# The first layer's paired sample steps: the prompt's scores, weight transposes and products in three places of a step instead of two

## The chip, the cores and the metric

The kernel runs on one core of a Trainium2 chip. The metric is the device time of one execution in microseconds (us). The engines are named as in the profile: PE (TensorE, its weight loads apart as PEld), DVE (VectorE), ACT (ScalarE), POOL (GpSimd) and SP (SyncE, here the queue that issues most DMAs; SPq is its sequencer).

## The reference

One inference step of a decoder with two layers, for a prompt group (512 tokens) and a sample group (8 sequences of 8 tokens, each with 2048 tokens in a paged cache). The first layer mixes by a pooling part and a differential attention, four heads, each with two score maps of 64 features:

```
def diff_attn_core(q, ks, vs, masks, lam, lam_init, subln_g):
    logits = jnp.concatenate([jnp.einsum('bqhmd,bkhmd->bhmqk', q, k) for k in ks], axis=-1).astype(jnp.float32) * (HD_B ** -0.5)
    logits = jnp.where(jnp.concatenate(masks, axis=-1), logits, -jnp.inf)
    p = jax.nn.softmax(logits, axis=-1)
    a = p[:, :, 0] - lam * p[:, :, 1]
...
        part = jnp.einsum('bhqk,bkhe->bqhe', a[..., off:off + n].astype(v.dtype), v)
...
    o = rmsnorm(o, subln_g) * (1.0 - lam_init)
```

The prompt attends to itself, causally, in blocks of 128 queries; the samples attend to their cache pages and to themselves. Then come the output projection, an MLP, a second layer (convolution and dilated window attention) and its MLP; these are not touched here.

## The kernel before

Each engine runs its own list of instructions in the order in which the program writes them; semaphores hold an instruction until another engine has done its part. There is no scheduler: what stands next in an engine's list waits, and all behind it on that engine waits too.

The stage of this case is the first layer's attention. The samples are taken in four pairs (j = 0 to 3), and each pair in nine blocks (i = 0 to 8): eight with two cache pages of each sample of the pair, that is four pages of 512 KB, and one with the new tokens. That makes 36 steps, m = 9j + i. On PE a step is: the sample scores (`scores`, L728), the key transposes of the next block's first two pages (`keys`, L714), the value products of the block before (`values`, L748), the key transposes of the next two pages (L714), then a piece of other work, and the transposes of the sample's own weights (`weights`, L736). In the step with i = 7 there are no next keys. DVE and ACT copy the transposed keys from PSUM (L1338 and L1932, every second page each, one PSUM bank for each engine), DVE takes the maximum of the scores (L1348 to L1354), ACT the exponentials (L1942) and the copy of the weights (L1950). SP loads the pages into a ring of four blocks (`kvring`, L431); a slot is free again when the values of the block four before are done.

The other work is the prompt's attention, in 16 items (4 heads by 4 query blocks; n = 4h + qt, and a query block has qt + 1 key blocks). Each item passes through PE three times: scores (L834, PSUM buffer `P0_SCORES`), transposes of the combined weights (L845), products (L852; both in PSUM bank 7). Between them DVE masks and reduces the scores (L1450, L1451), ACT takes the exponentials (L2008), DVE combines the two maps into one (`prompt_combine`, L1462 to L1466, semaphore `p0_a`), ACT copies the transposed weights (L2017, semaphore `p0_at`). DVE copies the result out (L1456) and ACT squares it (L2040).

Which item falls into which step is said by `beside(m, first, stage, last)`: item s runs in step m = first + 7 * s // 4. DVE has three such calls: output of n at first = 4, mask and maximum of s at first = 1, combine of n at first = 2. PE and ACT have before the change a `prompt_stage(s)` at first = 1 that holds the scores (on ACT the exponentials) of item s and, right behind them, the weights of item s - 1; PE's products stand at first = 4, ACT's squares too. In a step PE runs the product first, then the scores, then the weights.

Of the kernel before, what the change touches and what calls it, by code (L numbers as in the profile page):

```python
# [26 lines left out]
ACT = mybir.ActivationFunctionType  # L27
# [3 lines left out]
P = 128  # L31
# [111 lines left out]
def build(nc, a):  # L143

    with ExitStack() as ctx:
# [15 lines left out]
        def at(name, word, words, dt=F32):  # L161
            assert word + words <= total, (name, word + words, total)
            return nc.alloc_sbuf_tensor_at(name, [P, words], dt, offset=base + 4 * word)

        def tiles(t, n, first=0):
            return t[:, first * N:(first + n) * N].rearrange("p (k n) -> p k n", n=N)
# [23 lines left out]
        pk = tiles(proj, 16)  # L190
# [10 lines left out]
        ident, ones = cc("ident"), cc("ones")  # L201
# [32 lines left out]
        e4 = [[at(f"e4{u}{m}", W_W + 1024 * u + 512 * m, 512) for m in range(2)] for u in range(2)]  # L234
        pt_p0 = [at(f"pt_p0{i}", W_PROJ + 12 * N + 512 * i, 512) for i in range(2)]
# [44 lines left out]
        neg0 = stat0[:, 0:4].rearrange("p (u m) -> p u m", u=2)  # L280
        sum0 = stat0[:, 4:8].rearrange("p (u m) -> p u m", u=2)
# [37 lines left out]
        p0_s, p0_m, p0_e, p0_a, p0_t, p0_at, p0_pv, p0_o = (sem(f"p0_{n}") for n in  # L319
            ("s", "m", "e", "a", "t", "at", "pv", "o"))  # L320
# [77 lines left out]
        P0_SCORES, P0_WEIGHTS, P0_OUTPUT = pp[2], bank[7], bank[7][:, 0:P]  # L398
# [6 lines left out]
        def beside(m, first, stage, last):  # L405

            for s in range(last + 1):
                if m == first + 7 * s // 4:
                    stage(s)
# [227 lines left out]
        def _(pe):  # L637
# [175 lines left out]
            for i in range(4):  # L813
                last = pe.transpose(bank[6][:, P * i:P * i + 120], hist_tok[0:120, P * i:P * i + P],
                                    ident[0:120, 0:120])
            last.then_inc(hist_ps, 1)
            pe.wait_ge(acc_free, 2 + T_AB + 4)
            for i in range(4):
                last = pe.transpose(bank[7][:, P * i:P * i + P], pk[:, i, N - P:N], ident)
# [5 lines left out]
            token_major(0, pk[:, 8:12, :], pk[:, 12:16, :], 0)  # L825


            def prompt_stage(s):
                if s < 16:
                    h, qt = s // 4, s % 4  # L830
                    if s >= 1:
                        pe.wait_ge(p0_e, s)
                    for m in range(2):
                        last = pe.matmul(P0_SCORES[:, 512 * m:512 * m + P * (qt + 1)],  # L834
                                         pk[64 * m:64 * m + 64, 4 + h, P * qt:P * qt + P],
                                         pk[64 * m:64 * m + 64, 8 + h, 0:P * (qt + 1)], start=True, stop=True)
                    last.then_inc(p0_s, 1)
                if s >= 1:
                    n = s - 1
                    qt = n % 4  # L840
                    pe.wait_ge(p0_a, n + 1)
                    if n >= 1:
                        pe.wait_ge(p0_o, n)
                    for kb in range(qt + 1):
                        last = pe.transpose(P0_WEIGHTS[:, P * kb:P * kb + P], e4[n % 2][0][:, P * kb:P * kb + P], ident)  # L845
                    last.then_inc(p0_t, 1)

            def prompt_product(n):
                h, qt = n // 4, n % 4
# [6 lines left out]
            def mixer_product(g):  # L856

                pe.wait_ge(pm_ready, g + 1)
                if g == 0:
                    pe.wait_ge(p0_e, 16)  # L860
                else:
                    pe.wait_ge(mix_done, g)
                for h in range(2):
                    last = pe.matmul(halves[2][:, h, :], a_mix[:, P * g:P * g + P], pk[:, g, NH * h:NH * h + NH],
                                     start=True, stop=True)
                last.then_inc(mix_ps, 1)

            def head_columns(h):

                pe.wait_ge(sub_n, h + 1)  # L870
                if h == 0:
                    pe.wait_ge(p0_o, 16)
                elif h >= 2:
                    pe.wait_ge(sub_l, h - 1)
                for t in range(4):
                    last = pe.transpose(HEADS[h][:, P * t:P * t + P], pk[:, 4 + h, P * t:P * t + P], ident)
                last.then_inc(sub_t, 1)
# [3 lines left out]
            def combine_samples(part):  # L881

                pe.wait_ge(S0["fin"], part + 1)
                for b in (range(NB - 2), range(NB - 2, NB))[part]:
                    last = pe.matmul(bank[4][:, 32 * b:32 * b + 32], orun0[:, P * b:P * b + P], comb0[:, b, :],
                                     start=True, stop=True)
                last.then_inc(S0["fin_ps"], 1)

            def prompt_work(m):
                beside(m, 4, prompt_product, 15)  # L890
                beside(m, 1, prompt_stage, 16)
                if 28 <= m < 32:
                    mixer_product(m - 28)
                if m == 33:
                    head_columns(0)
                if m == 34:
                    pe.wait_ge(mix_done, 4)
                    combine_samples(0)
                    head_columns(1)
                if m == 35:  # L900
                    head_columns(2)
# [26 lines left out]
            pe.wait_ge(tk_done, 5)  # L928
            pe.wait_ge(tv_done, 5)
            sample_attention(prompt_work)  # L930


# [5 lines left out]
            for h in range(4):  # L938
                last = pe.matmul(bank[6][0:NS, h:h + 1], o_sq[:, h, :], ones[:, 0:1], start=True, stop=True)
# [910 lines left out]
        def _(act):  # L1850
            def split_hi(G, q, free=True):

                j = q % 2
                if j == 0:
                    act.wait_ge(raw_loaded[q // 2], G * 16 + 16)
                act.activation(whi_v[j], raw_v[q // 2][:, :, j, :], ACT.Copy).then_inc(whi_ready, 1)  # L1856
# [140 lines left out]
            dense(lambda i: i + 3, 1, last=True)  # L1997
            token_major(0)

            def prompt_stage(s):  # L2000
                if s < 16:
                    qt, u = s % 4, s % 2
                    nk = P * (qt + 1)
                    act.wait_ge(p0_m, s + 1)
                    if s >= 2:
                        act.wait_ge(p0_t, s - 1)
                    for m in range(2):
                        last = act.activation(e4[u][m][:, 0:nk], P0_SCORES[:, 512 * m:512 * m + nk], ACT.Exp,  # L2008
                                              bias=neg0[:, u, m:m + 1], accum_out=sum0[:, u, m:m + 1])
                    last.then_inc(p0_e, 1)  # L2010
                if s >= 1:
                    n = s - 1
                    nk = P * (n % 4 + 1)
                    act.wait_ge(p0_t, n + 1)
                    if n >= 2:
                        act.wait_ge(p0_pv, n - 1)
                    act.activation(pt_p0[n % 2][:, 0:nk], P0_WEIGHTS[:, 0:nk], ACT.Copy).then_inc(p0_at, 1)  # L2017

            def prompt_work(m):
                beside(m, 1, prompt_stage, 16)  # L2020
                beside(m, 4, prompt_square, 15)
                if 28 <= m < 32:
                    g = m - 28
                    act.wait_ge(mix_ps, g + 1)
                    act.activation(pk[:, g, :].rearrange("p (h c) -> p h c", h=2), halves[2], ACT.Copy,
                                   scale=gains[:, G_SCALE + g:G_SCALE + g + 1]).then_inc(mix_done, 1)
                    act.wait_ge(mix_done, g + 1)
                    act.activation(ohk[:, g, :], pk[:, g, :], ACT.Copy).then_inc(mix_hi, 1)
                if m == 31:
                    act.wait_ge(sub_v, 1)  # L2030
                    act.activation(r_h0, r_h0, ACT.Sqrt).then_inc(sub_r, 1)
                if m >= 33:
                    head_high(m - 33)
                if m == 33:
                    split_hi(T_OA // 4, 0)
# [7 lines left out]
            def head_high(h):  # L2043

                act.wait_ge(sub_t, h + 1)
                act.activation(ohk[:, 4 + h, 0:SEQ], HEADS[h], ACT.Copy,
                               scale=gains[:, G_HEAD:G_HEAD + 1]).then_inc(sub_h, 1)

            act.wait_ge(rows_out, 32)
            act.wait_ge(kout[0], 16)  # L2050
            act.wait_ge(kout[1], 16)
            sample_attention(samp0, prompt_work)
            split_hi(T_OA // 4, 1)
            act.activation(dummy_a, ident[:, 0:1], ACT.Sqrt)
# [366 lines left out]
```

## Time and profile before

| | |
|---|---|
| median of 3 runs | 1837.92 us (1835.81 to 1840.8) |
| the profiled execution | 1836.39 us, its span (first to last instruction) 1834.8 us |
| busy share of the span | PE 97%, PEld 90%, DVE 50%, ACT 32%, POOL 9% |
| mean granted clock of TensorE | 0.993 of full speed |
| stage 138 to 347 us: busy share of PE, DVE, ACT | 88%, 65%, 53% |

PE is almost always busy, so a microsecond in which it waits is a microsecond of the whole time, and the shares of the other engines say little. The stage of the change is the exception: there PE waits for others now and then, and it is there that the waits have to be read one by one. Its times (stage row) come from a table of busy times by stretch.

### The profile page before, as it was taken

The numbers are of one execution on the slowest core, as the hardware profiler recorded it, in microseconds if no ns is written. First come the engines' busy times: TensorE is split into PE (matmuls) and PEld (weight loads), VectorE is DVE, ScalarE is ACT, GpSimd is POOL, SyncE is SP. The second block draws the span as 40 slices with busy tenths as digits, with TensorE's granted clock in tenths as the row PEclk, the third lists the DMA queues.
The fourth block names the chain that finished last, engine by engine and source line by source line (L and its number), as shares of the span: only waits on it lengthen the run. The fifth ranks groups of instructions, "written<-read, shape, count | busy, mean of one in ns | idle before, by whom it ended". The sixth has DMA issues, their size and how long they took to land.

```text
span 1834.8 us, 37580 instructions
## 1 busy us (share of the span) xinstructions
PE 1774.8 (97%) x15399; PEld 1650.7 (90%) x15399; DVE 919.5 (50%) x1396; ACT 582.0 (32%) x1137; POOL 161.0 (9%) x224
## 2 busy tenths in 40 slices
PE   7998998999999999999999999999999999999998
PEld 6995666799999999999888888878789999999998
DVE  4336666646343443444544555478674534344354
ACT  4114555532122222231533443363223212222222
POOL 0710000230000000020000000003002000000001
PEclk9999999999999999999999999999999999999999
DMA  8219888436767677543367667733124676532321
GB/s 271 69 59 359 320 327 315 149 115 229 251 241 262 228 251 251 188 142 141 111 185 249 204 196 235 243 103 110 48 100 132 211 268 225 199 97 69 91 81 62
DMA packets 167165, 338.88 MB, mean 185 GB/s; under 512 B 9178, under 2 KB 116500, under 8 KB 165437
## 3 DMA queue, kind: packets, MB, share of 16 engines
q1 hardware_dynamic: 164691, 249.74, 40.7%
q0 software_dynamic: 2240, 87.41, 12.8%
q8 instruction: 87, 1.43, 0.3%
q14 instruction: 33, 0.27, 0.0%
q10 hardware_dynamic: 114, 0.03, 0.0%
HBM read 324.36 MB, written 100.19 MB: 231 GB/s over the span
## 4 chain that ended last, share of the span: by engine, by line
PE 88%; DVE 7%; ACT 2%; issue 1%; DMA 1%; SPq 1%; ACTq 0%; DVEq 0%
PE pp L654 54%; PE pp L964 16%; PE pp L714 3%; PE pp L1074 2%; PE pp L1121 2%; PE pp L1087 1%; PE pp L913 1%; PE pp L728 1%; PE pp L748 1%; PE pp L1102 1%; DVE stat L1605 1%; DVE pp L1603 1%; ACT e_p L2076 1%; DVE stat L1451 1%; PE pp L1146 1%
## 5 line engine op out<-in xcount | busy, mean ns | idle before, releaser
L1856 ACT ACTIVATE whi<-raw 128x1024 fp32r<-128x1024 f32 x208 | 220.6, 1061 | 841.9 <-PE pp L654 685.4
L654 PE MATMUL pp<-a_hi,whi 128*128 128x288 f32 x1280 | 276.2, 297 | 1.0 <-DVE zbuf L1272 0.7
L654 PE MATMUL pp<-a_hi,wlo 128*128 128x288 f32 x1280 | 274.5, 296 | 0.0
L654 PE MATMUL pp<-a_lo,whi 128*128 128x288 f32 x1280 | 274.4, 296 | 0.0
L1229 DVE TENSOR_TENSOR wlo<-raw,whi 128x1024 fp32r<-128x1024 f32 x208 | 256.1, 1231 | 35.9 <-ACT whi L1856 35.9
L654 PE MATMUL pp<-b_hi,whi 128*128 128x288 f32 x1152 | 246.8, 296 | 0.0
L654 PE MATMUL pp<-b_hi,wlo 128*128 128x288 f32 x1152 | 246.6, 296 | 0.0
L654 PE MATMUL pp<-b_lo,whi 128*128 128x288 f32 x1152 | 246.6, 296 | 0.0
L654 PEld LDWEIGHTS pp<-a_hi,whi 128*128 128x128 f32 x1280 | 206.8, 189 | 2.3 <-issue 1.6
L1288 DVE TENSOR_TENSOR x<-x,pp 128x576 f32 (+1 forms) x80 | 60.4, 755 | 292.9 <-PE pp L654 281.8
L654 PEld LDWEIGHTS pp<-a_lo,whi 128*128 128x128 f32 x1280 | 206.8, 189 | 0.0
L654 PEld LDWEIGHTS pp<-a_hi,wlo 128*128 128x128 f32 x1280 | 206.7, 189 | 0.0
L654 PEld LDWEIGHTS pp<-b_hi,whi 128*128 128x128 f32 x1152 | 185.7, 189 | 0.0
L654 PEld LDWEIGHTS pp<-b_lo,whi 128*128 128x128 f32 x1152 | 185.7, 189 | 0.0
L654 PEld LDWEIGHTS pp<-b_hi,wlo 128*128 128x128 f32 x1152 | 185.7, 189 | 0.0
L964 PE MATMUL pp<-a_hi,whi 128*128 128x288 f32 x768 | 184.5, 322 | 0.4 <-DVE proj L1544 0.4
L964 PE MATMUL pp<-a_hi,wlo 128*128 128x288 f32 x768 | 163.7, 295 | 0.0
L964 PE MATMUL pp<-a_lo,whi 128*128 128x288 f32 x768 | 163.5, 294 | 0.0
L964 PEld LDWEIGHTS pp<-a_hi,whi 128*128 128x128 f32 x768 | 118.7, 189 | 37.7 <-issue 36.7
L1272 DVE TENSOR_TENSOR zbuf<-pp,rnorm 128x576 f32<-128x576 f32 x64 | 48.5, 758 | 185.3 <-PE pp L654 185.2
L964 PEld LDWEIGHTS pp<-a_hi,wlo 128*128 128x128 f32 x768 | 123.0, 188 | 0.0
L964 PEld LDWEIGHTS pp<-a_lo,whi 128*128 128x128 f32 x768 | 122.9, 188 | 0.0
(283 smaller groups left out, 2133.0 us busy)
## 6 DMA issues: line engine op xcount, KB each, us to landing
kvring<-in_cache_b_kv SPq DMA_DIRECT2D x128, 512.0 KB, 5.6
out_new_d_sample<-in_cache_d_kv POOLq DMA_DIRECT2D x32, 2040.0 KB, 8.4
raw<-in_w_up SPq DMA_DIRECT2D x32, 1024.0 KB, 5.5
raw<-in_w_down SPq DMA_DIRECT2D x32, 1024.0 KB, 5.0
kring<-in_cache_d_kv SPq DMA_DIRECT2D x104, 256.0 KB, 3.1
vring<-in_cache_d_kv SPq DMA_DIRECT2D x104, 256.0 KB, 4.6
raw<-in_w_in_cd SPq DMA_DIRECT2D x24, 1024.0 KB, 5.3
out_new_d_sample<-in_cache_d_kv POOLq DMA_DIRECT2D x8, 2016.0 KB, 8.4
```

The source lines that it names most:

```text
L654: last = pe.matmul(acc_h[s][:, h, :], w[s][:, k, :], m[:, k, NH * h:NH * h + NH], start=(at_ == 0 and n == 0), stop=(at_ == KT_N - 1 and n ...
L714: last = pe.transpose(bank[p % 2][:, P * t:P * t + P], kv_v[i % 4][:, p, 0, P * t:P * t + P], ident)
L728: last = pe.matmul(SCORES[32 * t:32 * t + 32, 0:2 * P if i < NB0 - 1 else NS], staged[u][j % 2][:, 0, t, :], keys_, start=(u == 0), stop=( ...
L748: last = pe.matmul(OUTPUT[32 * t:32 * t + 32, P * u:P * u + P], pt_l0[i % 2][0:w, P * n + 32 * t:P * n + 32 * t + 32], v[:, P * t:P * t + ...
L913: last = pe.matmul(acc_h[T % 2][:, h, :], w[T % 2][:, k, :], m[:, k, NH * h:NH * h + NH], start=(k == 0 and n == 0), stop=(k == KT_N - 1 a ...
L964: last = pe.matmul(acc_h[s][:, h, :], w[s][:, k, :], m[:, k, NH * h:NH * h + NH], start=(k == 0 and n == 0), stop=(k == KT_N - 1 and n == 2))
L1074: last = pe.transpose(bk[:, P * t:P * t + P], kring1[j % NK][:, P * t:P * t + P], ident)
L1121: last = pe.matmul(S1_OUT[32 * t:32 * t + 32, :], pt_s1[0:w, P * n + 32 * t:P * n + 32 * t + 32], v[:, P * t:P * t + P], start=(n == 0), s ...
L1229: dve.tensor_tensor(wlo_v[j], raw_v[q // 2][:, :, j, :], whi_v[j].bitcast(F32), ALU.subtract).then_inc(wlo_ready, 1)
L1272: dve.tensor_tensor(z.rearrange("p (h c) -> p h c", h=2), acc_h[j], r_h, ALU.mult).then_inc(acc_free, 1)
L1288: dve.tensor_tensor(xt, xt, acc_h[q % 2], ALU.add).then_inc(acc_free, 1)
L1856: act.activation(whi_v[j], raw_v[q // 2][:, :, j, :], ACT.Copy).then_inc(whi_ready, 1)
```

## The change

`prompt_stage` is split on PE into `prompt_scores` (first = 1) and `prompt_weights` (first = 3), and on ACT into `prompt_exp` (first = 1) and `prompt_weights` (first = 3). The instructions, their waits and their increments are the same as before; DVE's code is not touched. In a step the order on PE is now product, scores, weights, and on ACT exponentials, weights, squares.

```diff
-            def prompt_stage(s):
-                if s < 16:
-                    h, qt = s // 4, s % 4
-                    if s >= 1:
-                        pe.wait_ge(p0_e, s)
...
-                if s >= 1:
-                    n = s - 1
-                    qt = n % 4
-                    pe.wait_ge(p0_a, n + 1)
-                    if n >= 1:
-                        pe.wait_ge(p0_o, n)
...
+            def prompt_scores(s):
+                h, qt = s // 4, s % 4
                 if s >= 1:
+                    pe.wait_ge(p0_e, s)
...
+            def prompt_weights(n):
+                qt = n % 4
+                pe.wait_ge(p0_a, n + 1)
+                if n >= 1:
+                    pe.wait_ge(p0_o, n)
+                for kb in range(qt + 1):
+                    last = pe.transpose(P0_WEIGHTS[:, P * kb:P * kb + P], e4[n % 2][0][:, P * kb:P * kb + P], ident)
+                last.then_inc(p0_t, 1)
...
             def prompt_work(m):
                 beside(m, 4, prompt_product, 15)
-                beside(m, 1, prompt_stage, 16)
+                beside(m, 1, prompt_scores, 15)
+                beside(m, 3, prompt_weights, 15)
...
+            def prompt_exp(s):
...
+            def prompt_weights(n):
+                nk = P * (n % 4 + 1)
+                act.wait_ge(p0_t, n + 1)
+                if n >= 2:
+                    act.wait_ge(p0_pv, n - 1)
+                act.activation(pt_p0[n % 2][:, 0:nk], P0_WEIGHTS[:, 0:nk], ACT.Copy).then_inc(p0_at, 1)
...
             def prompt_work(m):
-                beside(m, 1, prompt_stage, 16)
+                beside(m, 1, prompt_exp, 15)
+                beside(m, 3, prompt_weights, 15)
                 beside(m, 4, prompt_square, 15)
```

The changed file is a line shorter, so that L834, L845 and L852 of before are L833, L844 and L851 there, and on ACT L2008 and L2017 are L2007 and L2016. On PE, at the end of step m = 2 (scores of item 1; `e_93` holds the combined weights of item 0, `e_81` the sample's exponentials; in brackets the semaphores that a row waits for), before and now:

```order
 L714 MATMUL pp<-con,kvring_73 128x128 x3
-L834 MATMUL pp<-proj 128x256 [waits p0_e]
-L834 MATMUL pp<-proj 128x256
-L845 MATMUL pp<-con,e_93 128x128 [waits p0_a]
+L833 MATMUL pp<-proj 128x256 [waits p0_e]
+L833 MATMUL pp<-proj 128x256
 L736 MATMUL pp<-con,e_81 128x128 [waits sa0_e]
 L736 MATMUL pp<-con,e_81 128x128
```

The one transpose of item 0, with its wait for `p0_a`, is gone from between the scores and the sample weights. It stands at the end of step m = 3 on PE:

```order
 L714 MATMUL pp<-con,kvring_70 128x128 [waits sa0_kt_d]
 L714 MATMUL pp<-con,kvring_70 128x128 x3
+L844 MATMUL pp<-con,e_93 128x128 [waits p0_a]
 L736 MATMUL pp<-con,e_82 128x128 [waits sa0_e]
 L736 MATMUL pp<-con,e_82 128x128
```

The same happens to items 4, 8 and 12 (from step 9 to 10, 16 to 17, 23 to 24); for all other items the rows are those of before. On ACT, steps m = 16 and 17, before (`pt_l` are the sample's weights, `e_95` and `e_96` the exponentials of item 9, `pt_p_97` the copied weights of item 8, `rnorm` the square of item 7, `kt_l` the key copies):

```order
L1950 ACTIVATE pt_l_89<-pp 128x256 [waits sa0_pt_ps]
L2008 ACTIVATE e_95,stat_92<-pp,stat_92 128x256 [waits p0_t,p0_m]
L2008 ACTIVATE e_96,stat_92<-pp,stat_92 128x256
L2017 ACTIVATE pt_p_97<-pp 128x128 [waits p0_pv,p0_t]
L2040 ACTIVATE rnorm<-proj 128x128 [waits p0_o]
L1932 ACTIVATE kt_l_99<-pp 128x4x128 [waits sa0_kt_ps]
L1942 ACTIVATE e_81,samp_147<-pp,samp_147 128x64 [waits sa0_pt_ps,sa0_neg]
L1945 ACTIVATE samp_147<-samp_147 128x1
L1932 ACTIVATE kt_l_99<-pp 128x4x128 [waits sa0_kt_ps]
L1950 ACTIVATE pt_l_88<-pp 64x128 [waits sa0_pt_ps]
L1932 ACTIVATE kt_l_100<-pp 128x4x128 [waits sa0_kt_ps]
```

And the same rows of ACT with the change:

```order
L1950 ACTIVATE pt_l_89<-pp 128x256 [waits sa0_pt_ps]
L2007 ACTIVATE e_95,stat_92<-pp,stat_92 128x256 [waits p0_t,p0_m]
L2007 ACTIVATE e_96,stat_92<-pp,stat_92 128x256
L2040 ACTIVATE rnorm<-proj 128x128 [waits p0_o]
L1932 ACTIVATE kt_l_99<-pp 128x4x128 [waits sa0_kt_ps]
L1942 ACTIVATE e_81,samp_147<-pp,samp_147 128x64 [waits sa0_pt_ps,sa0_neg]
L1945 ACTIVATE samp_147<-samp_147 128x1
L1932 ACTIVATE kt_l_99<-pp 128x4x128 [waits sa0_kt_ps]
L1950 ACTIVATE pt_l_88<-pp 64x128 [waits sa0_pt_ps]
L2016 ACTIVATE pt_p_97<-pp 128x128 [waits p0_pv,p0_t]
L1932 ACTIVATE kt_l_100<-pp 128x4x128 [waits sa0_kt_ps]
```

The copy of the prompt's weights has moved from between the exponentials and the square of step 16 to the end of step 17.

## Rows read from the trace of the kernel before

**Rows 1.** Waits of PE, 135 to 350 us: in total, times, longest.

```profile
PE pp L845 <- DVE e L1466: 9.2, 4, 2.3
PE pp L728 <- DVE kt_l L1338: 5.6, 11, 0.9
PE pp L714 <- ACT kt_l L1932: 5.5, 10, 1.0
PE pp L714 <- DMA kvring<-in_cache_b_kv: 2.2, 2, 1.4
```

**Rows 2.** Timeline of PE, steps 2 to 4: start, duration, idle before and releaser.

```profile
155.29 0.70 PE L834 MATMUL pp<-proj 64*128 64x256 f32 x4
158.29 0.33 PE L845 MATMUL pp<-con,e 128*128 128x128 f32 x1 [2.29 <-DVE e L1466]
...
158.76 1.07 PE L728 MATMUL pp<-kt_l,q_st 128*32 128x256 f32 x16
...
161.80 1.09 PE L714 MATMUL pp<-con,kvring 128*128 128x128 f32 x8
...
163.77 1.07 PE L728 MATMUL pp<-kt_l,q_st 128*32 128x256 f32 x16 [0.66 <-DVE kt_l L1338]
```

**Rows 3.** Timeline of PE, around steps 9, 16 and 23.

```profile
194.08 0.70 PE L834 MATMUL pp<-proj 64*128 64x256 f32 x4
...
204.13 1.07 PE L728 MATMUL pp<-kt_l,q_st 128*32 128x256 f32 x16 [0.66 <-DVE kt_l L1338]
...
234.80 0.70 PE L834 MATMUL pp<-proj 64*128 64x256 f32 x4
...
238.28 0.43 PE L728 MATMUL pp<-qkv_s,q_st 128*32 128x64 f32 x16
...
244.20 1.07 PE L728 MATMUL pp<-kt_l,q_st 128*32 128x256 f32 x16 [0.77 <-DVE kt_l L1338]
...
276.43 0.70 PE L834 MATMUL pp<-proj 64*128 64x256 f32 x4
...
286.54 1.07 PE L728 MATMUL pp<-kt_l,q_st 128*32 128x256 f32 x16 [0.66 <-DVE kt_l L1338]
```

**Rows 4.** Timeline of DVE, a clean step (176 us), then steps 16 and 17.

```profile
176.24 0.42 DVE L1352 TENSOR_REDUCE samp<-pp 128x1 f32<-128x256 f32 x1
...
176.97 0.69 DVE L1338 COPY kt_l<-pp 128x512 f32<-128x512 f32 x1
...
236.02 0.69 DVE L1451 TENSOR_REDUCE stat<-pp 128x2 f32<-128x512 f32 x1
...
237.39 0.35 DVE L1466 SCALAR_TENSOR_TENSOR e<-e,stat,e 128x128 f32<-128x128 f32 x1
238.77 0.23 DVE L1348 TENSOR_TENSOR pp<-pp,con 128x64 f32<-128x64 f32 x1 [1.03 <-PE pp L728]
```

**Rows 5.** Timeline of ACT, steps 16 and 17.

```profile
238.38 0.38 ACT L1950 ACTIVATE pt_l<-pp 128x256 f32<-128x256 f32 x1 [4.00 <-PE pp L736]
238.66 0.47 ACT L2008 ACTIVATE e<-pp,stat 128x256 f32<-128x256 f32 x1
...
239.56 0.28 ACT L2017 ACTIVATE pt_p<-pp 128x128 f32<-128x128 f32 x1
...
240.01 0.61 ACT L1932 ACTIVATE kt_l<-pp 128x512 f32<-128x512 f32 x1
```

**Rows 6.** Busy us (instructions) by stretch, then PE's granted clock, DMA busy share, GB/s.

```profile
158.40:163.00 4.60, 4.60 (x69) 3.35 (x69) 2.05 (x6) 3.20 (x11) 0.00 (x0) 1.00 1.03 410
197.00:203.00 6.00, 5.92 (x67) 4.23 (x68) 1.88 (x6) 3.13 (x13) 0.00 (x0) 0.72 0.05 20
138.00:189.57 51.57, 42.78 (x591) 30.25 (x589) 32.79 (x79) 24.70 (x76) 1.43 (x4) 1.00 0.98 363
```

**Rows 7.** The cache page loads, 135 to 350 us: from issue to landing.

```profile
DMA to landing us min/median/max: 3.4/5.5/7.8
```

**Rows 8.** Waits of the load queue, 130 to 350 us: in total, times, longest.

```profile
SPq L429 <- PE pp L748: 46.3, 22, 9.6
```

More of the change, by code:

```diff
@@ L825, in _ @@
             token_major(0, pk[:, 8:12, :], pk[:, 12:16, :], 0)
-            def prompt_stage(s):
-                if s < 16:
-                    h, qt = s // 4, s % 4
-                    if s >= 1:
-                        pe.wait_ge(p0_e, s)
[L833 to L837, printed above, removed]
-                if s >= 1:
-                    n = s - 1
-                    qt = n % 4
-                    pe.wait_ge(p0_a, n + 1)
-                    if n >= 1:
-                        pe.wait_ge(p0_o, n)
-                    for kb in range(qt + 1):
-                        last = pe.transpose(P0_WEIGHTS[:, P * kb:P * kb + P], e4[n % 2][0][:, P * kb:P * kb + P], ident)
-                    last.then_inc(p0_t, 1)
+            def prompt_scores(s):
+                h, qt = s // 4, s % 4
+                if s >= 1:
+                    pe.wait_ge(p0_e, s)
+                for m in range(2):
+                    last = pe.matmul(P0_SCORES[:, 512 * m:512 * m + P * (qt + 1)],
+                                     pk[64 * m:64 * m + 64, 4 + h, P * qt:P * qt + P],
+                                     pk[64 * m:64 * m + 64, 8 + h, 0:P * (qt + 1)], start=True, stop=True)
+                last.then_inc(p0_s, 1)
+            def prompt_weights(n):
[6 more added lines that the diff above has]
+                last.then_inc(p0_t, 1)
             def prompt_product(n):
@@ L1998, in _ @@
             token_major(0)
[L2000 to L2010, printed above, removed]
-                if s >= 1:
[L2012 to L2017, printed above, removed]
+            def prompt_exp(s):
+                qt, u = s % 4, s % 2
+                nk = P * (qt + 1)
+                act.wait_ge(p0_m, s + 1)
+                if s >= 2:
+                    act.wait_ge(p0_t, s - 1)
+                for m in range(2):
+                    last = act.activation(e4[u][m][:, 0:nk], P0_SCORES[:, 512 * m:512 * m + nk], ACT.Exp,
+                                          bias=neg0[:, u, m:m + 1], accum_out=sum0[:, u, m:m + 1])
+                last.then_inc(p0_e, 1)
+            def prompt_weights(n):
[4 more added lines that the diff above has]
+                act.activation(pt_p0[n % 2][:, 0:nk], P0_WEIGHTS[:, 0:nk], ACT.Copy).then_inc(p0_at, 1)
             def prompt_work(m):
-                beside(m, 1, prompt_stage, 16)
+                beside(m, 1, prompt_exp, 15)
+                beside(m, 3, prompt_weights, 15)
                 beside(m, 4, prompt_square, 15)
```

## The prediction

> **What bounds the kernel now.** I read the page first: TensorE (PE) is busy for 97% of the span, so the time is PE's time plus whatever PE waits. Then I went to the stage that the change touches, the 36 steps of the first layer's paired sample attention, some 138 to 347 us into the span, and asked whom PE waits for there. The answer is short [rows 1]: the largest entry is the transposes of the prompt's weights (L845), which wait for VectorE's (DVE's) combination of the two softmaxes (L1466), 9.2 us in all, but only four times and never longer than 2.3 us. All other waits are many small ones: 5.6 us for DVE's copies of transposed keys, 5.5 us for ScalarE's (ACT's) copies, 2.2 us for cache pages, two times, both in the first pair.
>
> Next the timeline of PE around one such wait, step m = 2 [rows 2]. After the scores at 155.29 PE stands still for 2.29 us; a single transpose starts at 158.29, behind it the sample weights (L736, two more transposes of that size), at 158.76 the next step's sample scores (L728), then the first half of the key transposes (L714), the value products (L748) and at 161.80 the second half of the keys. The reader should see that the stalled transpose is one instruction, and that nothing behind it on PE needs it. The other three places look alike: four waits of up to 2.3 us make the 9.2 us; their scores stand in [rows 3].
>
> Why these four: step m holds scores s when m = 1 + 7s // 4, and the weights of item n sat beside scores n + 1. DVE combines item n at m = 2 + 7n // 4. For n = 0, 4, 8, 12 both fall into the same step (m = 2, 9, 16, 23); for the other twelve DVE is a step ahead. In the same step DVE must first mask and reduce the new scores and then run the four combining instructions: at m = 16 the reduction starts at 236.02 and the last combining instruction, 0.35 us, at 237.39 [rows 4], so it ends at 237.74; until then PE, whose scores began at 234.80 [rows 3], cannot go on.
>
> **The change part by part.** With 3 + 7n // 4 the weights come at m = 3, 4, 6, 8, 10, 11, 13, 15, 17, ...; before, they came at 2, 4, 6, 8, 9, 11, 13, 15, 16, .... So in spite of its wide diff the change moves only four PE transposes (n = 0, 4, 8, 12, one 128x128 each, the causal first block of each head) and four ACT copies, each by one step. No instruction is added, none removed, no DMA issue moves on any queue, and DVE, POOL and SP keep their order. Products, squares and DVE's outputs come no earlier than m = 4 + 7n // 4, still a step behind the moved work.
>
> *What PE does instead of waiting.* I replay the step [rows 2], each term being the distance of two starts. Scores to the sample weights 0.64 us (their 0.70 us less an overlap of 0.06); weights to L728 0.31 (two thirds of the 0.47 us between 158.29 and 158.76); L728, first keys and products together 3.04; second keys to the next step's L728 1.97, a distance in which PE already waits for DVE's copy of the last page (the 5.6 us above), so that the moved transpose, the third third, 0.16 us, hides in it (without that cover it costs 0.6 us in all). Sum 5.96 us, from the scores of step m to L728 of step m + 2. Now it takes 8.48 us at m = 2, 10.05 at m = 9, 9.40 at m = 16 and 10.11 at m = 23 [rows 2, 3].
>
> *Is DVE or ACT late next?* DVE still has the combine ahead of its next work. At m = 9 the combine ends, in the same distance from the scores as at m = 16, at 197.02; the next step's maximum and key copy follow (0.05 us to start, 0.73 from the maximum to the copy and 0.69 for the copy, as in a clean step [rows 4], some 0.15 until PE sees it: 198.64), and PE would want that bank half a group (0.51 us) into the second keys, at 194.08 + 0.64 + 0.31 + 3.04 + 0.51 = 198.58. So 0.07 us is lost and DVE is just in time. ACT no longer stands idle for 4.00 us ahead of L1950 [rows 5]; its exponentials still wait for DVE's reduction, but their 0.90 us (238.66 to 239.56) and the square end before the copy of the first key page is wanted. Its own moved copy (L2017, 0.28 us) now follows L1950 one step later, while PE runs the next L728 and keys, for which ACT has to wait anyway; without that cover 1.1 us in all. At m = 16 it is tighter. Step 17 has only 64 sample columns, so L728 lasts 0.43 us instead of 1.07 [rows 2, 3]: PE wants the second half of the keys at 238.15, ACT's copy (L1932), now at 240.01, could start at about 237.95, lasts 0.61 and releases PE at 238.7, and DVE's copy, after the combine and the three short instructions that begin with L1348, frees the other bank at about 239.4. I charge 0.75 us there, a sum of 6.06 us.
>
> *What the clock gives back.* The replay holds PE at full speed. In before, the granted clock is 1.00 after the first stall, but 0.72 over the 6 us after the second [rows 6], and much the same after the third and the fourth, for which that row stands: of the two levels, 2.4 and 1.2 GHz, PE had the lower for a part of that time, after an idle time of 2.29 us, and lost 0.28 x 6 = 1.68 us. That is why the steps at m = 9 and 23 take 1.6 us longer than that at m = 2. With PE busy there I take the clock to stay up; unknown, bounded by 0 and 1.68 us at each of three places.
>
> *Where the cache pages bind.* At m = 2 the transfers run without a break: 410 GB/s and a busy share of 1.03 between 158.4 and 163 us [rows 6]. A page lands 3.4 to 7.8 us after its issue [rows 7], and in this full stretch near the upper end, while PE would reach the next blocks 2.5 us sooner. I estimate that 1.0 of the 2.52 us goes to waits for pages (bounds 0 and 2.52) and take 1.5. At the other three places the page loads wait for PE instead: the load queue stood 46.3 us in all for value products (L748) to free a slot of the ring [rows 8]. What frees a slot sooner issues the next load sooner.
>
> So the gains are m = 2: 1.5; m = 9: 10.05 - 5.96 - 0.07 = 4.0; m = 16: 9.40 - 6.06 = 3.3; m = 23: 10.11 - 5.96 - 0.07 = 4.1; together 12.9 us. All after the stage is PE's own work and shifts with it, the weight loads of the output projection too, since the queue waits for sample scores. The profiled execution took 1836.39 us (span 1834.8): less 12.9 that is 1823.5. The median of the runs is 1.5 us above the profiled one; between 1823.5 and 1825.0 I say 1824.
>
> **The rivals.**
>
> A, the forecast: the stalls go, the clock holds. 1821.5 (every bound on the good side: 2.5 + 4.1 + 4.1 + 4.2 = 14.9 us) to 1827. Chance 0.63.
>
> B, the clock falls all the same. Short waits in a row can do it: at m = 16 two remain, and in before the clock had fallen after a wait of only 2.29 us. All three drops stay: 12.9 - 5.0 = 7.9 us, 1828.5 to 1830. For it: the level after the first stall shows that a stall and a drop do not go strictly together. Against: over the first 51 us of the stage the mean is 1.00 [rows 6], with the first stall and many of the small waits in it. Chance 0.18.
>
> C, the cache pages become the bound. If in each of the three later pairs PE met what it met in the first, 2.2 us [rows 1], 6.6 us would go: a gain of 6.3, about 1830.5. For it: a block of four pages, 2.1 MB, takes 5.1 us at 410 GB/s [rows 6], and a clean step lasts as little as 5.0 us (158.76 to 163.77) [rows 2]. Against: the queue's 46.3 us of waiting for PE. Chance 0.09. The Trainium skill, page "DMA: Bandwidth & Descriptors", section "Where 436 GB/s comes from", says that transfers between HBM and SBUF are held by the HBM side to about 358 GB/s per core; by that figure a block would take, as an estimate, 5.9 us, longer than a step, and this rival would be the likeliest. This case's trace does not agree: it moves 410 GB/s there.
>
> D, nothing: DVE is the real pace, and PE waits in the next step for the copies behind the combine what it did not wait before. The margin of 0.07 us above is thin; but DVE itself stands idle for 1.03 us ahead of L1348, waiting for PE [rows 4], so it can follow. 1836 to 1838. Chance 0.06.
>
> E, slower: PE runs ahead of the pages in all twelve tight blocks of the later pairs (blocks 4 to 7 of each, whose slot is free only when PE is done with the block four before), waits 1.1 us for each (the mean of the two waits in [rows 1]) and, at every second, loses another 1.65 us to the clock: 13.2 + 9.9 - 12.9 = 10 us, 1847. It decides from the point where these losses pass 18.4 us. Chance 0.04.
>
> **How the numbers follow.** About 5.5 us (0.3%) is what can be told from no change here. Faster: A, B and most of C, 0.89; same: D and the rest of C, 0.07; slower: E, 0.04. The range leaves out D and E and the worst of C: 1821 to 1831.
>
> **What would show it.** Right: no wait of PE for L1466; from the scores of m = 9 and 23 to L728 two steps on 6.0 us, at m = 16 6.1, at m = 2 about 7; granted clock near 1.00 after each; the stage some 13 us shorter; the rest of the span as long as now. Wrong: waits for cache pages that grow past 2.2 us (C), a clock of 0.7 after m = 9, 16 or 23 (B), or key copies of DVE and ACT that hold PE as long as the combine did (D).

## The result, and the profile after

The changed kernel took 1822.14 us, the median of 4 executions (1821.89 to 1822.48), against 1837.01 (1835.81 to 1840.8, also 4) for the kernel before: a ratio of 0.9916 [0.9899, 0.9933], so 14.9 us less in the medians, where the prediction had 13 to 14. Timed again later, it took 1822.97 (5 executions) against 1837.71 (8): 0.9925 [0.9911, 0.9939].

The waits of PE in the stage after, from 135 to 336 us: in total, times, longest.

```profile
PE pp L714 <- ACT kt_l L1932: 5.8, 11, 1.0
PE pp L728 <- DVE kt_l L1338: 5.7, 11, 0.9
PE pp L714 <- DMA kvring<-in_cache_b_kv: 3.3, 4, 1.1
```

The entry that led [rows 1], 9.2 us for DVE's combination, is gone; no other took its place. The copies of keys cost what they cost before (5.8 and 5.7 us against 5.5 and 5.6), which is what speaks against rival D. Only the waits for cache pages grew, from 2.2 us in two times to 3.3 us in four.

The timeline of PE after, at steps 2 to 4 and around steps 9, 16 and 23 (the lines behind the edit are one lower than before: scores L833, prompt weights L844):

```profile
153.45 0.70 PE L833 MATMUL pp<-proj 64*128 64x256 f32 x4
154.08 0.44 PE L736 MATMUL pp<-con,e 128*128 128x128 f32 x2
154.45 1.07 PE L728 MATMUL pp<-kt_l,q_st 128*32 128x256 f32 x16
156.34 1.09 PE L714 MATMUL pp<-con,kvring 128*128 128x128 f32 x8 [0.81 <-DMA kvring<-in_cache_b_kv]
157.36 1.08 PE L748 MATMUL pp<-kvring,pt_l 128*32 128x128 f32 x32
158.91 1.09 PE L714 MATMUL pp<-con,kvring 128*128 128x128 f32 x8 [0.47 <-DMA kvring<-in_cache_b_kv]
159.84 0.27 PE L844 MATMUL pp<-con,e 128*128 128x128 f32 x1
159.94 0.38 PE L736 MATMUL pp<-con,e 128*128 128x128 f32 x2
160.87 1.07 PE L728 MATMUL pp<-kt_l,q_st 128*32 128x256 f32 x16 [0.55 <-DVE kt_l L1338]
...
191.23 0.70 PE L833 MATMUL pp<-proj 64*128 64x256 f32 x4
191.87 0.44 PE L736 MATMUL pp<-con,e 128*128 128x128 f32 x2
192.24 1.07 PE L728 MATMUL pp<-kt_l,q_st 128*32 128x256 f32 x16
...
196.20 0.27 PE L844 MATMUL pp<-con,e 128*128 128x128 f32 x1
...
197.24 1.07 PE L728 MATMUL pp<-kt_l,q_st 128*32 128x256 f32 x16 [0.55 <-DVE kt_l L1338]
...
227.92 0.70 PE L833 MATMUL pp<-proj 64*128 64x256 f32 x4
...
231.81 1.06 PE L714 MATMUL pp<-con,kvring 128*128 128x128 f32 x8 [0.42 <-ACT kt_l L1932]
...
233.74 1.07 PE L728 MATMUL pp<-kt_l,q_st 128*32 128x256 f32 x16 [0.66 <-DVE kt_l L1338]
...
265.98 0.70 PE L833 MATMUL pp<-proj 64*128 64x256 f32 x4
...
271.98 1.07 PE L728 MATMUL pp<-kt_l,q_st 128*32 128x256 f32 x16 [0.55 <-DVE kt_l L1338]
```

Behind the scores the sample weights (L736) now follow at once, and the moved transpose (L844) stands a step later, without a wait. From the scores to L728 two steps on the step now takes 197.24 - 191.23 = 6.01 us at m = 9 and 271.98 - 265.98 = 6.00 at m = 23, where it took 10.05 and 10.11; 7.42 at m = 2, with 1.28 us of page waits in it (8.48 before); and 233.74 - 227.92 = 5.82 at m = 16 (9.40 before). The four steps together are 12.8 us shorter. From the first sample scores to those of the last step the stage lasts 189.07 us; before, 203.30. That is 14.2 of the 14.5 us between the two spans (1834.8 and 1820.3). Some 1.3 us of the 14.2 are not the change's: in this profile of the kernel before the clock fell once more at the end of the stage, behind waits that the change leaves as they are (busy time by stretch, columns as below):

```profile
328.00:331.00 3.00, 1.52 (x14) 1.08 (x14) 1.29 (x3) 2.97 (x7) 0.38 (x1) 1.00 0.93 348
331.00:335.00 4.00, 4.00 (x40) 2.56 (x44) 1.61 (x3) 1.41 (x5) 4.00 (x4) 0.57 0.28 89
```

From there (330.98) to the last sample scores it took 11.63 us, in the changed kernel 10.31. The changed kernel had a fall of its own, 0.72 from 325 to 331 us, but nearly all of it behind its last sample scores (326.74), where this count ends.

Busy time by stretch after, over the steps that the change touches: busy us (instructions) of PE, PEld, DVE, ACT, POOL, then PE's granted clock, DMA busy share and GB/s.

```profile
156.00:162.00 6.00, 4.65 (x68) 3.48 (x69) 4.05 (x12) 2.80 (x9) 0.00 (x0) 1.00 1.03 408
231.00:237.00 6.00, 4.93 (x72) 3.58 (x63) 4.93 (x15) 3.22 (x12) 0.00 (x0) 1.00 1.03 415
150.00:280.00 130.00, 121.42 (x1709) 87.71 (x1702) 96.50 (x241) 73.96 (x241) 2.34 (x8) 1.00 0.95 366
```

From 150 to 280 us, which takes in all four places, the granted clock is 1.00, where 0.72 stood behind the second stall before [rows 6]. The load queue still waits for PE, 32.7 us in all where it was 46.3 [rows 8]:

```profile
SPq L429 <- PE pp L748: 32.7, 20, 6.3
```

### The profile page after: what moved, and what is told of

It reads as the page before. It is cut to its first block, busy times and chain, and to the rows that moved or that the text cites. A ratio compares the mean times of both kernels' runs of the same rounds, so it can differ in the third digit from the quotient of the medians.

```text
span 1820.3 us, 37580 instructions
## 1 busy us (share of the span) xinstructions
PE 1765.6 (97%) x15399; PEld 1643.6 (90%) x15399; DVE 919.0 (50%) x1396; ACT 583.0 (32%) x1137; POOL 161.3 (9%) x224
## 3 DMA queue, kind: packets, MB, share of 16 engines
q0 software_dynamic: 2240, 87.41, 12.8%
## 4 chain that ended last, share of the span: by engine, by line
PE 89%; DVE 5%; ACT 3%; issue 1%; SPq 1%; DMA 1%; ACTq 0%; DVEq 0%
PE pp L654 54%; PE pp L964 16%; PE pp L714 3%; PE pp L1074 2%; PE pp L1121 2%; PE pp L1087 1%; PE pp L913 1%; PE pp L748 1%; PE pp L728 1%; ACT e_p L2076 1%; PE pp L990 1%; PE pp L1102 1%; PE pp L1146 1%; DVE rnorm L1259 1%; PE pp L833 1%
```

## The experiments

The theory: PE stood behind one transpose whose input DVE combines late in the same step; with it a step later the stalls go, and the clock that three of them cost. Open were what the clock's part is and to which stalls it belongs, whether ACT's part of the change matters, and what the waits for cache pages in the first pair cost. Below, "step m" is the time from the scores of m to L728 of m + 2.

**The kernel before, once more.** No edit.

> The kernel before, unchanged, profiled once more. Theory (the four stalls and the clock that falls behind them are this program's own): the same four waits for L1466 of 2.29 us, 9.2 us in all, and the granted clock near 0.7 for some 6 us behind those of steps 9, 16 and 23; scores of step 9 to L728 of step 11 again 10.0 us, of step 23 to 25 again 10.1 us. Rival (where the clock falls is chance, from one execution to the next): the same waits, but falls behind other stalls, so that single steps come out at 8.5 instead of 10.0 us. The lead of 1.4 us that the changed kernel has ahead of the stage: by the theory chance, so this execution differs from the first by a microsecond or two there.

It took 1834.27 us, again with four stalls, 9.2 us in all. The stretches of 6 us behind them in its profile (columns as above):

```profile
157.50:163.50 6.00, 5.90 (x67) 4.42 (x68) 1.97 (x6) 2.84 (x11) 0.00 (x0) 0.72 0.93 369
197.50:203.50 6.00, 4.88 (x73) 3.56 (x77) 3.09 (x10) 3.86 (x14) 0.00 (x0) 1.00 0.17 47
237.00:243.00 6.00, 5.57 (x68) 4.29 (x68) 2.45 (x8) 3.54 (x14) 0.83 (x4) 0.72 0.99 399
278.00:284.00 6.00, 5.31 (x63) 3.34 (x64) 2.12 (x7) 2.99 (x12) 0.00 (x0) 0.72 0.80 325
```

This time the clock fell behind the first, third and fourth stall and held behind the second, which waits as long as it did (the timeline of PE in the same profile, steps 2 and 9):

```profile
154.60 0.70 PE L834 MATMUL pp<-proj 64*128 64x256 f32 x4
...
164.64 0.64 PE L728 MATMUL pp<-kt_l,q_st 128*32 128x256 f32 x8 [0.66 <-DVE kt_l L1338]
...
194.97 0.70 PE L834 MATMUL pp<-proj 64*128 64x256 f32 x4
...
197.97 0.33 PE L845 MATMUL pp<-con,e 128*128 128x128 f32 x1 [2.29 <-DVE e L1466]
...
203.44 0.85 PE L728 MATMUL pp<-kt_l,q_st 128*32 128x256 f32 x12 [0.66 <-DVE kt_l L1338]
```

Step 9 took 203.44 - 194.97 = 8.47 us where it had taken 10.05, step 2 took 164.64 - 154.60 = 10.04 where it had taken 8.48. So the falls do not belong to steps 9, 16 and 23, as the prediction had them, but come to one stall or another of the same kernel; one costs 10.05 - 8.47 = 1.6 us. For the third and fourth stall of the first profile these are the stretches:

```profile
238.00:243.00 5.00, 5.00 (x66) 3.94 (x65) 2.01 (x6) 2.79 (x13) 0.82 (x4) 0.66 1.02 408
279.00:285.00 6.00, 5.57 (x63) 3.72 (x64) 1.89 (x6) 2.98 (x12) 0.00 (x0) 0.72 0.73 296
```

**ACT's part alone.** PE as before; on ACT the exponentials and the copy of the weights apart:

```diff
-                beside(m, 1, prompt_stage, 16)
+                beside(m, 1, prompt_exp, 15)
+                beside(m, 3, prompt_weights, 15)
```

> Only ACT's part of the change: its four copies of the prompt's weights a step later, PE's list as before. Theory (all of the gain is PE's wait): no change, 1837 us, four waits of 2.3 us for L1466. Rival (ACT's shorter steps 2, 9, 16 and 23 bring a part of it): up to 4 x 0.3 = 1 us faster.

1835.56 us (1832.6 to 1837.33, 10 executions) against 1836.61 (18), ratio 0.9995 [0.9986, 1.0005]: no difference, within 2.6 us faster and 0.9 slower. The four waits for L1466 are there, 9.2 us, and the clock fell behind steps 2, 16 and 23 again:

```profile
157.00:163.00 6.00, 6.00 (x68) 4.54 (x69) 1.98 (x5) 2.79 (x10) 0.00 (x0) 0.72 0.90 360
197.00:203.00 6.00, 5.06 (x74) 3.68 (x78) 3.08 (x10) 3.97 (x14) 0.00 (x0) 1.00 0.22 51
236.30:242.30 6.00, 5.57 (x68) 4.36 (x68) 2.45 (x8) 3.47 (x14) 0.82 (x4) 0.72 1.01 407
277.00:283.00 6.00, 5.02 (x60) 3.06 (x61) 2.13 (x6) 2.82 (x11) 0.00 (x0) 0.72 0.87 350
```

So moving ACT's four copies brings nothing that can be told by itself; the gain needs PE's part. PE's part without ACT's was not run.

**The combination first.** PE and ACT as before; DVE runs its four combining instructions ahead of the mask and reduction of the new scores:

```diff
                 beside(m, 4, prompt_output, 15)
+                beside(m, 2, prompt_combine, 15)
                 beside(m, 1, prompt_stage, 15)
-                beside(m, 2, prompt_combine, 15)
```

> PE and ACT as before; in DVE's other work of a step the combine stands ahead of the mask and reduction of the new scores. Theory (the combine is late because it is queued behind mask and reduction, 1.1 us, which wait for PE's scores): the combine then waits only for the output copy, PE's wait falls from 2.3 to about 0.8 us at steps 9, 16 and 23 and about 1.1 us at step 2, 3.5 in all, and with waits that short the clock stays up: 1837 - 5.7 - 4.9 = 1826 to 1827; ACT's exponentials come about 1.1 us later, which may give 1 to 2 us back. Rival (DVE is simply a step too late, whatever its order): waits of 2 us and more remain, 1835 to 1837.

1826.24 us (1822.81 to 1828.86, 4 executions), ratio 0.9941 [0.9918, 0.9964]. The wait for L1466 fell from 9.2 to 3.5 us (4 times, longest 1.2). The timeline of PE at step 9:

```profile
194.14 0.33 PE L845 MATMUL pp<-con,e 128*128 128x128 f32 x1 [0.78 <-DVE e L1466]
```

and that of DVE:

```profile
193.73 0.35 DVE L1466 SCALAR_TENSOR_TENSOR e<-e,stat,e 128x128 f32<-128x128 f32 x1
194.46 0.69 DVE L1451 TENSOR_REDUCE stat<-pp 128x2 f32<-128x512 f32 x1
```

With the combine ahead of the reduction the transpose waits 0.78 us instead of 2.29. What PE waited for was thus DVE's order of work, as [rows 4] were read. The steps took 7.37, 6.96, 6.58 and 6.97 us, and the clock did not fall behind any of the four.

**Half of the change, twice.** Only two of the four transposes move, on PE and ACT; here items 0 and 8 (steps 2 and 16), then with (4, 12) in place of (0, 8) the items of steps 9 and 23 (the edit is against the changed kernel):

```diff
-                beside(m, 3, prompt_weights, 15)
+                for n in range(16):
+                    if m == (3 if n % 4 or n in (0, 8) else 2) + 7 * n // 4:
+                        prompt_weights(n)
```

> The change for items 0 and 8 alone (steps 2 and 16); items 4 and 12 stay in steps 9 and 23. Theory (each place has its own price, that of the two profiles: 1.1 us at step 2, 3.6 at step 16, 4.0 at step 9, 4.1 at step 23): two waits of 2.3 us remain, the clock falls behind both, 1837 - 4.7 = 1832. Rival (the falls of the clock sit at times of their own and not behind these stalls): the two stalls cost 2.4 us each and no more, 1837 - 12.8 + 4.8 = 1829.

> The change for items 4 and 12 alone (steps 9 and 23); items 0 and 8 stay in steps 2 and 16. Theory (each place has its own price): 4.0 + 4.1 us gained, 1829 us, a wait of 2.3 us at step 2 with the clock up and one at step 16 with the clock near 0.7 behind it. Rival (the falls of the clock sit at times of their own): the stall at step 16 costs 2.4 us and no more, and 1827 us.

Items 0 and 8: 1831.66 us (9 executions), ratio 0.9966 [0.9955, 0.9977]. Items 4 and 12: 1825.71 (4) against 1838.14 (9), ratio 0.9942 [0.9924, 0.996]. In each the two unmoved stalls stood, 4.6 us, and the moved steps were short. Busy time by stretch behind the unmoved ones, at steps 9 and 23 with items 0 and 8 moved:

```profile
195.50:201.50 6.00, 6.00 (x68) 4.13 (x69) 1.85 (x5) 3.23 (x13) 0.00 (x0) 0.72 0.03 11
275.00:281.00 6.00, 5.27 (x78) 3.82 (x82) 3.21 (x10) 3.85 (x14) 0.00 (x0) 1.00 0.71 250
```

and at steps 2 and 16 with items 4 and 12 moved:

```profile
157.70:163.70 6.00, 5.27 (x78) 3.82 (x82) 3.21 (x10) 3.68 (x12) 0.00 (x0) 1.00 0.84 302
233.20:239.20 6.00, 5.19 (x85) 3.78 (x86) 3.82 (x11) 3.54 (x14) 0.83 (x4) 1.00 1.03 409
```

One fall in four. The unmoved steps took 10.05 (fall) and 8.48 us, and 8.47 and 7.89. So a stall without a fall costs 8.48 - 6.00 = 2.5 us at step 23, as much at step 9 (8.47 in the second profile of the kernel before), and 7.89 - 5.82 = 2.1 at step 16. Of the expectations the first time came true (1832), but not its reason, a fall behind each stall; the second came 3 us below its time (1829), with no fall behind its two stalls where one was expected. Moving items 4 and 12 brought 10.7 us by the ratio (of 1838.14, with an interval of 7 to 14), items 0 and 8 6.2 (of 1836.61, 4 to 8): each pair brings a part, and the parts lie in the order of the prediction's terms (8.1 and 4.8), though the two intervals touch between 7 and 8.

**The pages first.** The changed kernel, and on SP's queue the stores of the new V rows, which stood with those of the K rows ahead of the first pair's page loads, come behind these loads:

```diff
-                each_pair(sp, pair)
+                pair(0)
+                store_tokens(0, a["new_bkv_prompt"], a["new_bkv_sample"], 0, (1,))
+                with sp.Fori(1, NP - 1) as j:
+                    pair(j)
+                pair(NP - 1)
...
-            store_tokens(0, a["new_bkv_prompt"], a["new_bkv_sample"], 0)
+            store_tokens(0, a["new_bkv_prompt"], a["new_bkv_sample"], 0, (0,))
```

> The changed kernel, and on the load queue the stores of the first layer's V rows moved from ahead of the cache pages to behind the last page load of the first pair. Theory (at step 2 the change gained 1.1 instead of 2.5 us because the pages of the first pair come late): the 3.3 us in which PE waits for pages in the first pair go, step 2 takes 6.0 instead of 7.4 us, 1819 us. Rival (the transfers are saturated there, so the pages land as late as before): the waits stay near 3 us, 1822 us.

1822.78 us (1819.12 to 1824.1, 5 executions): no lower than the changed kernel's 1822.14, although the page waits fell to 1.1 us. Its executions spread over 5 us, and the lowest, 1819.12, is the profiled one, in which PE even ran at the lower clock for some of 136 to 143 us. It was run again beside the changed kernel itself on the same chip:

> The changed kernel, timed beside the next run on one chip. Theory (the four places give 8 to 9 us without the clock and some 1.6 us more for every fall of the clock that they spare, 2 to 3 in an execution): 12 to 14 us below the median of before, 1822 to 1825 us, and in the profile no fall of the clock between steps 2 and 23. Rival (the 14.9 us of the first timing are the size, and part of it comes from elsewhere): 15 us or more below.

> The changed kernel with the stores of V behind the first pair's page loads, once more, beside the changed kernel on the same chip. Theory (the pages of the first pair were what was left at step 2): step 2 again 6.0 to 6.1 us, waits for pages 0 to 1.1 us instead of 3.1 to 3.3, 1 to 3 us faster than the changed kernel. Rival (what is gained there is lost to the clock or to later waits): the same time within 1 us.

The changed kernel: 1822.97 us (1822.46 to 1824.39, 5 executions), with page waits of 3.2 us. With the pages first: 1820.77 (1816.87 to 1821.63, 5), ratio to the kernel before 0.9902 [0.9887, 0.9918]. All five executions are below all five of the changed kernel, the medians by 2.2 us, and the stage in the profile is 186.75 instead of 189.27 us. Its waits of PE for pages, 135 to 347 us:

```profile
PE pp L718 <- DMA kvring<-in_cache_b_kv: 1.2, 4, 0.5
```

Its step 2 took 6.01 us (timeline of PE; the scores are L837 here, L728 is L732):

```profile
153.28 0.70 PE L837 MATMUL pp<-proj 64*128 64x256 f32 x4
...
159.29 1.07 PE L732 MATMUL pp<-kt_l,q_st 128*32 128x256 f32 x16 [0.55 <-DVE kt_l L1342]
```

What is left of the first pair's page waits is thus worth some 2.5 us of the stage. In the whole time the second round shows 2.2 us and the first none; over both, the ten executions have a median of 1821.1 us and the ten of the changed kernel 1822.7, with ranges that overlap. Two of the four waits, 0.6 us together, stand in the third pair (260.87 and 263.44), where the changed kernel has none.

**The changed kernel, profiled once more.** No edit.

> The changed kernel, profiled once more. Theory: steps 9 and 23 6.0 us, step 16 5.8 us, step 2 7.4 us, no wait for L1466, and the granted clock 1.00 from step 2 to step 30; what lies ahead of the stage and behind it differs by a microsecond or two from the first profile, each by a stretch at the lower clock. Rival (the clock in the stage was luck): one or two falls within the stage, 1.6 us each.

1823.66 us; steps 6.90, 6.01, 5.83 and 6.00, page waits 3.1 us, stage 189.23 us. In the profile of the timed rounds step 2 took 6.07 us with the same page waits, because the longest came a step earlier, outside it (timeline of PE):

```profile
155.23 1.09 PE L714 MATMUL pp<-con,kvring 128*128 128x128 f32 x8 [1.01 <-DMA kvring<-in_cache_b_kv]
```

**Both at once.** The changed kernel with DVE's combination first, as above.

> The changed kernel with DVE's combine ahead of mask and reduction. Theory (with the weights a step later PE no longer waits for the combine, so its place in DVE's list is free of price, and the later reduction only delays ACT): 1822 to 1824 us, no wait for L1466, more of the small waits of key transposes for ACT. Rival (DVE's order still binds): 2 us or more faster.

1827.07 us (1825.84 to 1828.02, 5 executions), ratio 0.9942 [0.9929, 0.9956]: 4 to 5 us slower than the change alone. On DVE the reduction now comes behind the combine, and ACT, in the changed order too, starts its exponentials only then (timeline of ACT):

```profile
194.41 0.47 ACT L2007 ACTIVATE e<-pp,stat 128x256 f32<-128x256 f32 x1 [1.04 <-DVE stat L1451]
...
195.61 0.59 ACT L1932 ACTIVATE kt_l<-pp 128x512 f32<-128x512 f32 x1
```

In the timeline of ACT of the changed kernel the same exponential waits 0.45 us:

```profile
193.18 0.47 ACT L2007 ACTIVATE e<-pp,stat 128x256 f32<-128x256 f32 x1 [0.45 <-DVE stat L1451]
...
194.38 0.59 ACT L1932 ACTIVATE kt_l<-pp 128x512 f32<-128x512 f32 x1
```

So the key copy that PE needs next is late, and steps 9, 16 and 23 take 6.41 us each, 1.4 more in all. The direction was expected, the size was not. The rest may go with the clock: its five executions had a mean granted clock of 0.9944, the ten of the changed kernel 0.9967, and 0.0023 x 1827 = 4.2 us, an estimate. That the small added waits make the clock fall more often is not shown: in the profile the clock is 1.00 from 150 to 280 us, behind all of them, and its one fall within the stage (0.80 from 314 to 322 us) stands where the waits are those of the changed kernel.

## Why the prediction was right, point by point

**The stall and its cause: right.** The four waits for L1466 are gone, and with the combine ahead of the reduction they shrink from 9.2 to 3.5 us while nothing is moved on PE. The other twelve items keep their places, as the order had shown. The four steps are 8.48 + 10.05 + 9.40 + 10.11 us before and 7.42 + 6.01 + 5.82 + 6.00 after, 12.8 us less where the terms made 12.9; that it comes so near is in part luck: step 2 gave 0.4 us less than its term and step 16 0.3 more.

**Steps 9 and 23: right.** 6.01 and 6.00 us, and 6.00 to 6.18 in the two further profiles, where 5.96 + 0.07 was worked out (0.06 by the prediction's own figures, 198.64 - 198.58). DVE is just in time: its copies hold PE no longer than before.

**Step 16: a little mis-sized.** The 0.75 us charged for late key copies is 0.42 in the row at 231.81, and the step 5.82 us, not 6.06. The term was 3.6 us rather than 3.3.

**Step 2: right within its bounds.** Page waits of 0.81 and 0.47 us stand in it, where 1.0 had been put; the gain is 1.06 us in the first profile, and step 2 took 6.07 to 7.42 us in three profiles, by where the page waits happened to fall. From the first sample scores of the stage to those of step 5 the changed kernel took 28.8 to 29.0 us in its three profiles, and 25.9 in the second one with the pages first, at whose step 2 nothing is left of page waits.

**The clock: sum right, places wrong.** The step that failed is "at m = 9, 16 and 23". Over the five profiles with unmoved stalls (twice the kernel before, ACT alone, the two halves) 16 of them waited 2.29 us, and behind 10 the clock fell: 3, 3, 3, 1 and 0. Which ones varies. Each fall costs some 1.5 us, where 1.68 had been read from the rows, and behind moved or shortened places there was none. So the four stalls cost without the clock 2.5 + 2.5 + 2.1 at steps 9, 23 and 16 and 1.1 to 1.6 at step 2, together 8.2 to 8.7 us. On top come the falls: 2.5 on the mean of the 16 waits, 3.8 us, or three, 4.5 us, as in every profile that had all four stalls. That makes 12 to 13 us, an estimate. The stage agrees: 201.6 us in the second profile of the kernel before and with ACT alone, and 189.1 to 189.3 in three profiles after, 12.3 to 12.6 less; the first profile, with 203.3, had the further fall at its end.

**"The rest of the span as long as now": right in the profiles, open in the medians.** Span less stage is 1631.5 and 1631.0 us in the two profiles of the kernel before, and 1631.2, 1632.9 and 1631.5 in the three of the changed one. These executions took 1835.3 and 1822.7 us on the mean, 12.7 less, and both of those before lie below the median of their kernel. The medians differ by 14.7 to 14.9 us, so some 2 us of them come from executions that left no profile. The granted clock has room for them: its mean was 0.9930 over 35 executions of the kernel before and 0.9967 over ten of the changed one, 0.0037 x 1835 = 6.8 us by estimate, of which the falls behind the four stalls make 3.8 to 4.5. Where those executions lose the rest is not shown.

**The rivals.** B did not come: no fall in any moved place. Its premise, that short waits in a row can do it, fits a fall elsewhere: waits of 0.89, 0.72 and 0.23 us stand ahead of the one at 331 us in the first profile of the kernel before, and in its second profile the same waits had none behind them. C did not come: in three profiles of the changed kernel all page waits lie in the first pair, and the queue still waits 32.7 us for PE. How near it was shows in two other runs, where the third pair waits 0.6 us (pages first) and 0.7 us (items 0 and 8) for pages. The Trainium skill's figure of about 358 GB/s per core (page "DMA: Bandwidth & Descriptors", section "Where 436 GB/s comes from"), by which C would have been likeliest, is not the limit here, with one core running: the page loads ran at 408 and 415 GB/s with a busy share of 1.03 after the change; the measurement decides. D is excluded by the unchanged waits for key copies, E by the time.

## What to carry to other kernels

On an engine that works in order, one small instruction whose input is produced late in the same step holds back everything behind it; find the step in which producer and consumer collide (here every fourth item of a schedule with a period of 7/4) and move the consumer a step, if something else covers it there. Moving the producer up instead brought less by the medians (a ratio of 0.9941 against 0.9916, with intervals that overlap), and doing both passed a delay on: ACT's exponentials waited 0.6 us longer in such a step, and 4 to 5 us of the gain were gone. Judge such a wait by the whole step, from one anchor to the next, in more than one profile, since the clock adds to some waits and not to others of the same length.

## What the runs showed of the hardware that had not been expected

Waits of PE of the same length, 2.29 us, at the same place of the same kernel are followed by the lower clock in one execution and not in the next: 10 of 16, with some 8.5 us for the step when it held and 9.9 to 10.1 when it fell (steps 2, 9 and 23). Where it fell, the mean over the 6 us behind was 0.72 nearly every time. A fall need not stand behind a wait of that length: the one at 331 us came behind three waits of less than 0.9 us each, with the engine busy for 1.52 of the 3 us before. Two stalls in a kernel instead of four had 1 and 0 falls each, too few to say that fewer stalls mean fewer falls per stall.
